# Gate and up products of the feed-forward blocks: from token rows to feature rows

## What is computed

```python
def swiglu(x, w1, w3, w2):                 # x (256, 1024); w1, w3 (1024, 2816); w2 (2816, 1024)
    return (jax.nn.silu(x @ w1) * (x @ w3)) @ w2
```

## Time and profile before

| | us |
|---|---|
| median of 3 runs | 1553.24 |
| the profiled execution, its own time | 1553.27 |
| span of its trace | 1551.3 |
| TensorE (PE) busy | 1491.5 (96%) |
| VectorE (DVE) busy | 875.4 (56%) |
| ScalarE (ACT) busy | 690.7 (45%) |
| GpSimd (POOL) busy | 169.5 (11%) |
| mean DMA rate | 177 GB/s |

### The profile page before, as it was taken

How to read it: one execution, slowest core, us unless ns; L and a number is a source line. 1 busy time by engine, 2 the same in 40 slices (tenths; PEclk the granted TensorE clock), 3 DMA queues, 4 the chain that set the end, 5 groups by cost and what they waited for, 6 DMA issues and landing times.

```text
span 1551.3 us, 20410 instructions
## 1 busy us (share of the span) xinstructions
PE 1491.5 (96%) x7720; PEld 1252.6 (81%) x7720; DVE 875.4 (56%) x1049; ACT 690.7 (45%) x840; POOL 169.5 (11%) x169
## 2 busy tenths in 40 slices
PE   6999998899999999999999999999999999899997
PEld 5987786688887888879978888878888887688886
DVE  3557665555456544567755445655454667564445
ACT  4345454434444444454434444364444467444442
POOL 1042110200000000110021000300000325500000
PEclk9999999999999999999999999999999999999999
DMA  6654463665555655565567556556555440365551
GB/s 220 218 173 151 150 200 109 196 216 188 189 190 166 200 189 189 170 206 177 170 210 237 184 184 193 174 164 217 189 189 189 149 156 29 109 217 189 188 186 60
DMA packets 198875, 274.54 MB, mean 177 GB/s; under 512 B 9632, under 2 KB 158240, under 8 KB 198560
## 3 DMA queue, kind: packets, MB, share of 16 engines
q1 hardware_dynamic: 194160, 256.16, 51.2%
q0 software_dynamic: 4512, 17.31, 3.2%
q10 hardware_dynamic: 144, 0.26, 0.0%
HBM read 272.38 MB, written 1.31 MB: 176 GB/s over the span
## 4 chain that ended last, share of the span: by engine, by line
PE 89%; DVE 5%; ACT 2%; POOL 1%; issue 1%; DMA 1%; SPq 0%; DVEq 0%; ACTq 0%
PE ps L621 28%; PE ps L623 28%; PE ps L622 28%; PE ps L960 1%; PE ps L662 1%; POOL big L2550 1%; DVE tmp L1859 1%; ACT big L1686 1%; DMA raw<-in_w_in 1%; DVE st_lo L1798 0%; PE ps L1026 0%; PE ps L1141 0%; DVE stats L1847 0%; DVE wlo L1776 0%; DVE tmp L1841 0%
## 5 line engine op out<-in xcount | busy, mean ns | idle before, releaser
L1776 DVE TENSOR_TENSOR wlo<-raw,whi 128x2048 fp32r<-128x2048 f32 x233 | 533.4, 2292 | 345.3 <-ACT whi L1284 344.4
L1284 ACT CAST whi<-raw 128x2048 fp32r<-128x2048 f32 x243 | 459.9, 1895 | 248.6 <-PE ps L623 246.6
L621 PE MATMUL ps<-whi,st_hi 128*128 128x512 f32 (+4 forms) x1352 | 527.9, 390 | 13.5 <-DVE wlo L1776 6.4
L623 PE MATMUL ps<-whi,st_lo 128*128 128x512 f32 (+4 forms) x1352 | 518.9, 384 | 0.0
L622 PE MATMUL ps<-wlo,st_hi 128*128 128x512 f32 (+4 forms) x1352 | 518.1, 383 | 0.0
L621 PEld LDWEIGHTS ps<-whi,st_hi 128*128 128x128 f32 (+1 forms) x1352 | 254.2, 188 | 64.8 <-DVE wlo L1776 7.6
L623 PEld LDWEIGHTS ps<-whi,st_lo 128*128 128x128 f32 (+1 forms) x1352 | 253.9, 188 | 50.7
L622 PEld LDWEIGHTS ps<-wlo,st_hi 128*128 128x128 f32 (+1 forms) x1352 | 254.6, 188 | 46.9 <-issue 0.2
L621 PE MATMUL ps<-whi,hid_hi 128*128 128x512 f32 x400 | 156.1, 390 | 0.0
L623 PE MATMUL ps<-whi,hid_lo 128*128 128x512 f32 x400 | 155.8, 390 | 0.0
L622 PE MATMUL ps<-wlo,hid_hi 128*128 128x512 f32 x400 | 155.6, 389 | 0.0
(11 more groups left out here) (237 smaller groups left out, 1115.5 us busy)
## 6 DMA issues: line engine op xcount, KB each, us to landing
raw<-in_ffn_w SPq DMA_DIRECT2D x264, 512.0 KB, 4.3
raw<-in_w_gate_up SPq DMA_DIRECT2D x44, 512.0 KB, 4.7
raw<-in_w_in SPq DMA_DIRECT2D x32, 512.0 KB, 4.8
raw<-in_sgu_w_in SPq DMA_DIRECT2D x32, 512.0 KB, 4.6
raw<-in_w_down SPq DMA_DIRECT2D x22, 512.0 KB, 4.0
raw<-in_sgu_w_out SPq DMA_DIRECT2D x16, 512.0 KB, 4.7
raw<-in_kv_w SPq DMA_DIRECT2D x12, 512.0 KB, 4.0
raw<-in_w_proj_attn SPq DMA_DIRECT2D x8, 512.0 KB, 4.3
```

Source lines behind the costliest of these rows:

```text
L621: pe.matmul(o, a[0], b[0], start=start, stop=False)
L623: return pe.matmul(o, a[1], b[0], start=False, stop=stop)
L1284: act.copy(whi[:, s, 0:n], raw[:, s, 0:n]).then_inc(whi_ready, 1)
L1776: dve.tensor_tensor(wlo[:, s, 0:n], raw[:, s, 0:n], whi[:, s, 0:n].bitcast(F32), ALU.subtract).then_inc(wlo_ready, 1)
```

## The change

Step 0 stays as it is. In steps 1 to 10 of each block the weights become stationary and the turned input moves. A step has four tiles of 128 hidden features (gate and up, for features 0 to 127 and 128 to 255), a bank each (7, 6, 4, 5). The high and the low part of the input now lie in one tile `st`, so that one matmul of `whi` over 512 columns, twice 256 tokens, writes high x high into the left half of the bank and high x low into the right half. A matmul of `wlo` over 256 columns adds to the left half. DVE then adds the halves of each bank (a reduction over pairs, `tile_sum`). The result has features on partitions, so steps 1 to 10 have no transposes: silu, product, high and low part are made in SBUF from `silu` and `hidden`.

```diff
-        st_hi = sb("st_hi", [P, 16, S], F32R)
-        st_lo = sb("st_lo", [P, 16, S], F32R)
+        st = sb("st", [P, 2, 16, S], F32R)
+        st_hi = st[:, 0, :, :]
+        st_lo = st[:, 1, :, :]
...
@@ TensorE, gate_up(i)
-                        for tb, key in enumerate(up):
+                        for t in range(4):
+                            key = ("tile", n, t)
...
-                                pe.wait_ge(bank_read[b], c + i)
+                                pe.wait_ge(bank_read[b], c + i - 1)
+                            f0 = FC * (t % 2) + P * (t // 2)
+                            both = bank(key).rearrange("p (a b) -> p a b", a=2)
                             for k in range(4):
-                                mm = product(bank(key), [x[:, 4 * half + k, tb * P:tb * P + P] for x in (st_hi, st_lo)],
-                                             [x[:, k, :] for x in w], half == 0 and k == 0, half == 1 and k == 3)
+                                x = 4 * half + k
+                                if x == 0:
+                                    pe.matmul(both, w_hi[:, k, f0:f0 + P], st[:, :, x, :], start=True, stop=False)
+                                mm = pe.matmul(bank(key)[:, 0:S], w_lo[:, k, f0:f0 + P], st_hi[:, x, :],
+                                               start=False, stop=False)
+                                if x:
+                                    mm = pe.matmul(both, w_hi[:, k, f0:f0 + P], st[:, :, x, :], start=False,
+                                                   stop=x == KD - 1)
...
@@ TensorE, the loop and the last step
                 with pe.Fori(2, FSTEPS - 1) as i:
                     gate_up(i, u0 + 2, i - 1)
                     down(i - 1, u0 + 4, i - 1)
-                    turn(i)
...
                 gate_up(i, u0 + 2, i - 1)
-                turn_last(0)
-                pe.wait_ge(*read(hid, i - 1))
+                pe.wait_ge(hid_ready, hidden0 + i - 1)
                 w_before = down_weights(u0 + 4, i - 1)
                 down_block(w_before, hid_hi, hid_lo, 0)
-                turn_last(1)
                 w_last = down_weights(u0 + 3 * FSTEPS - 1, 0)
                 last = [x[:, 8:10, :] for x in (st_hi, st_lo)]
-                pe.wait_ge(*read(("hid_last", n, 0)))
+                pe.wait_ge(hid_ready, hidden0 + i + 1)
                 down_block(w_last, *last, 0, end=True)
                 down_block(w_before, hid_hi, hid_lo, 1).then_inc(w_used, 1)
-                pe.wait_ge(*read(("hid_last", n, 1)))
...
@@ ACT
+                def gate_rows(i):
+                    for f in range(2):
+                        act.wait_ge(*read(("tile", n, 2 * f), i - 1))
+                        act.activation(silu[:, f, :], silu[:, f, :], ACT.Silu).then_inc(silu_ready, 1)
...
+                def hidden_rows(i):
+                    act.wait_ge(hidden_ready, 2 * (FSTEPS - 1) * n + 2 * i)
+
+                    act.wait_ge(w_used, u0 + 2 + 3 * i)
+                    act.copy(hid_hi[:, :, :], hidden[:, :, :]).then_inc(hi_rounded, 1)
...
@@ DVE
+                def tile_sum(i, t):
...
+                    dve.tensor_reduce((silu, hidden)[t % 2][:, t // 2, :], view(bank(key)[:, 0:1], (1, S), (S, 2)), AX_X,
+                                      ALU.add).then_inc(*is_read(key))
```

More of the change, by code:

```diff
@@ L382, in plan_ffn @@
         def plan_ffn(n):
[L383 to L387, removed]
+            plan(("up", n, 0), 4)
+            plan(("up", n, 1), 5, unit=first["ffn", n] + 1)
+            plan(("hid", n), 0, split=True)
+            for t, b in enumerate((7, 6, 4)):
+                plan(("tile", n, t), b, times=FSTEPS - 1)
+            plan(("tile", n, 3), 5, times=FSTEPS - 1, unit=first["ffn", n] + 3)
+            plan_split(("hidden", n), FSTEPS - 2)
+            for f in range(2):
+                plan_split(("hid_last", n, f))
             for tb, h in ((0, 0), (0, 1), (1, 0)):
@@ L962, in turn @@
                     mm.then_inc(*is_full(hid))
[L964 to L970, removed]
                 by_block([(u0 + half, 4, 512, 4 * half, [bank(key) for key in up], up, half == 0, half == 1)
                           for half in range(2)], st=name, src=src)
-                gate_up(1, u0 + 2, 0, between=lambda: turn(0))
+                gate_up(1, u0 + 2, 0, between=turn)
                 for key in (k for pair in ykeys for k in pair):
@@ L1480, in swiglu, with gate_out, hidden_last, hidden_out @@
                 u0 = first["ffn", n]
[L1482 to L1500, removed]
+                def gate_out(tb):
+                    act.wait_ge(*full(("up", n, tb)))
+                    act.activation(silu[:, tb, :], bank(("up", n, tb))[:, 0:FC], ACT.Silu).then_inc(silu_ready, 1)
+                def gate_rows(i):
+                    for f in range(2):
+                        act.wait_ge(*read(("tile", n, 2 * f), i - 1))
+                        act.activation(silu[:, f, :], silu[:, f, :], ACT.Silu).then_inc(silu_ready, 1)
+                def hidden_last(f):
+                    act.wait_ge(hidden_ready, 2 * (FSTEPS - 1) * (n + 1) - 1 + f)
+                    act.copy(st_hi[:, 8 + f, :], hidden[:, f, :]).then_inc(hi_rounded, 1)
+                def hidden_out():
+                    act.wait_ge(*full(("hid", n)))
                     act.copy(hid_hi[:, :, :].rearrange("p a b -> p (a b)"), bank(("hid", n))).then_inc(hi_rounded, 1)
+                def hidden_rows(i):
+                    act.wait_ge(hidden_ready, 2 * (FSTEPS - 1) * n + 2 * i)
+                    act.wait_ge(w_used, u0 + 2 + 3 * i)
+                    act.copy(hid_hi[:, :, :], hidden[:, :, :]).then_inc(hi_rounded, 1)
                 upto(u0 + 1)
@@ L1524, in swiglu @@
                 upto(last)
-                gate_out(FSTEPS - 1)
-                hidden_last(0)
+                gate_rows(FSTEPS - 1)
+                for f in range(2):
+                    hidden_last(f)
                 upto(last + 1)
-                hidden_last(1)
             def second_block():
@@ L2105, in swiglu @@
                     split(*at(u0 + 5, i - 1))
-                    hidden_in(i)
+                    tile_sum(i, 0)
+                    tile_sum(i, 1)
+                    tile_sum(i, 2)
+                    hidden_rows(i, 0)
+                    tile_sum(i, 3)
+                    hidden_rows(i, 1)
                     split(*at(u0 + 6, i - 1))
-                    hidden_out(i)
+                    hidden_low(i)
+                    dve.wait_ge(hid_ready, FSTEPS * n + i)
                 nxt[0] = u0 + 3 * FSTEPS - 2
                 last = u0 + 3 * FSTEPS - 1
+                i = FSTEPS - 1
+                upto(last - 1)
+                tile_sum(i, 0)
                 upto(last)
-                hidden_in(FSTEPS - 1)
-                hidden_last(0)
+                tile_sum(i, 1)
+                tile_sum(i, 2)
+                hidden_rows(i, 0)
+                tile_sum(i, 3)
+                hidden_rows(i, 1)
+                for f in range(2):
+                    hidden_last(f)
                 upto(last + 1)
-                hidden_last(1)
             swiglu(0)
```

69 lines of the change are left out of this document (43 added, 26 removed).

## The result

| | before, us | after, us |
|---|---|---|
| median (lowest to highest), 5 runs each | 1553.24 (1552.99 to 1554.45) | 1559.39 (1558.73 to 1562.56) |
| the profiled execution, its own time | 1553.27 | 1562.53 |
| span of its trace | 1551.3 | 1560.7 |

The ratio is 1.0042, with a 95% interval of 1.0031 to 1.0053: 6 us slower, where 12.7 us faster was forecast. First the page of the profile and the chain of waits of the changed kernel, against the earlier trace rows.

A forecast was written before the change was run, and what follows sets the result against it. TensorE's own stream of products was taken as the bound. Products +10.7, turns -22.1 and block ends -1.3 made -12.7 us on 1553.3, so 1540.6 us; the range was 1537 to 1549.

The forecast's parts named there:

- Part 1: gate_up products in a step: 32 long and 32 short replace 48 long, 0.21 us more a step, 10.7 us more overall.
- the point of decision at 8 ns a product: Extra cost per long product at which the forecast gain is used up: 12.7 us / 1600.
- Part 2: Transposes of steps 1 to 9 in each block go: 45 turns at 0.49 us, 22.1 us less.
- Part 3: Other engines inside a step: operands ready some 5 us early, DVE's reductions of 0.69 us hidden and costed at nothing.
- The rival of longer sums: DVE's reductions take up to 0.96 us; hidden in steps, 4 us more at block ends, about 1545; 15%.
- Part 4: End of a block: both last turns go, 0.54 us, given back in blocks 1 and 2; together 1.3 us less.
- T: The end of gate_up(10) in a block, 649.67 in block 1 of the kernel before.
- two pieces: Long products' moving operand in two stretches costs two starts, 13 ns each, 21.3 us, 1562 us; 7%.
- loads not hidden: Loads of 16 more stationary operands a step cost 89 us, about 1620; 2%.
- cover gone: Inside steps, DVE or the ring of slots lags over 5 us and TensorE waits: 1553 or some us more; 4%.

The follow-up runs named there:

- experiments 9: Changed kernel with each 512-column product of gate_up made as two of 256 with the same stationary operand; 1571.83 us, ratio 1.0110.
- experiment 10: Changed kernel with POOL waiting for DVE's normalisation before its second split, and gate_up's long and short products in runs of sixteen; 1547.28 us, ratio 0.9959.
- experiment 6: Changed kernel with each of the four reductions in a loop step done twice, the copy into a scratch tile; 1560.5 us.
- experiment 1: Changed kernel with POOL splitting the next stage's second unit only after DVE finished the normalised values of token block 0; 1550.02 us, ratio 0.9967.
- experiment 11: Changed kernel with POOL's second split waiting for DVE's normalisation, products in runs of sixteen, but pairs in each block's last step; 1542.00 us, ratio 0.9925.
- 5: Changed kernel with long gate_up products moving 512 neighbouring values of st_hi instead of two stretches, leaving out high x low; 1558.75 us, single run.

## Why the prediction was wrong

**Part 1, mis-sized.** "32 x 0.2267 + 32 x 0.1200 = 11.09 us" took two prices from streams of one length each. Both hold in such streams (experiments 9, 10). In the order of the change each of 28 runs of short products costs 7 ns besides: 0.20 us a step, 10 us in 50 steps. I had seen the place ("the same point holds for anything that the change between long and short products costs"), set 2 ns for it in the range only, on 1600 changes where there are 28 x 50 = 1400, and the point of decision at 8 ns a product was nearly reached.

**Part 2, right.** `gate_up` takes 11.28 us (524.78 to 536.06) and `down` 5.46, and nothing of the step is left for a turn. A turn was a little cheaper than forecast: the mean step of 16.80 leaves 0.48 us for it, so 45 of them give 21.7 us and not 22.1. (16.82 - 16.32 would be 0.50, and not 0.49.)

**Part 3, right.** Sums of 0.68 us, for 0.69, hidden with room to double them (experiment 6). The rival of longer sums falls.

**Part 4, right up to its conclusion.** Low parts were ready at T + 2.4 (forecast 2.65), POOL's root at T + 9.4 (9.8), the first turned piece at T + 10.7, as said. Then the step that failed: "so in blocks 1 and 2 ... the next turned piece comes near T + 10.7, as before ..., and the 0.54 us are given back". It stopped at the first piece. I followed POOL's split and root by their place in the queue but not what a split does to the engine beside it: the first one now ended inside DVE's pair L1867, and the second one, which comes 0.5 us sooner with the turns gone, fell on the pair L1871 that it had just missed. It costs 4.4 and 4.9 us in the two blocks, 9.2 in all, by the distances of experiment 1; the other 1.7 of the 10.9 stay with POOL's wait in place. The pair's 1.42 us stood in the earlier trace rows; the second split did not, since I had followed POOL only as far as the root.

Together: 10 + 9.2 us explain the 18.8 from 1540.6 to 1559.4. With nearly all of both taken out (experiment 11) the change measures 12 us faster than before, close to the 12.7 forecast: the gain of the turns was there, and was paid away twice. The unlikely ones stay refuted: two pieces (5), loads not hidden (0.120 us with a load each, 9), cover gone (6).

The Trainium skill, "SBUF — State Buffer", section "Who interferes with whom", says that a DVE instruction with two SBUF inputs and a GpSimd instruction that reads SBUF take turns, the later one blocked for the whole of the first. The traces agree: pairs that take 1.42 or 1.54 us alone took 5.68, 5.53 and 3.62 (L1871, L1863, L1859) and ended within 1.4 us after a split's end, while L1849, with one operand in PSUM, keeps its 0.69 us during the split of 657.04.

## What to carry to other kernels

When an instruction in a queue is moved, follow everything behind it in every queue that it releases, until that queue idles, and lay each piece's new place over the other engines' work: 0.7 us decided here over four to five a block, and the same collision cost nothing where TensorE had other work. Prices of instructions measured in uniform streams did not add up in the mixed one here: look for a row of the mixture, or give the change its own bounds. Where one engine's instruction holds up another's, as POOL's split does DVE's pair here, a deliberate wait can pay, even if one then starts later.

## What the runs showed of the hardware

- Going from fp32r products of 256 columns to ones of 512, each with its own stationary operand, costs about 20 ns in long runs: the next five long products take 0.228 to 0.235 us instead of 0.227, 25 ns together, and the first two short ones after long ones 0.113 and 0.119 instead of 0.120 (experiment 10; the same in 9).
- DVE's `scalar_tensor_tensor` with two SBUF operands stands still beside a POOL `tensor_tensor` on SBUF: 5.68 us for 1.42. TensorE idled 3.6 us for it, and then had the lower clock level (products 0.43 us apart instead of 0.23) for 3.4 us. The lower level stands at this place of blocks 1 and 2 in all six traces with the collision, for 3.4 or 6.8 us, and in none of the eight without.
- A reduction from PSUM over pairs, 512 values in and 256 out, takes 0.68 us, the same as 512 in and 2 out (0.69): the values in set its time.
